# A filter network laid out on 128 partitions, its arrays the first load and its biases inside the vector of constants

## The reference, cut to what matters

```python
HY_EMB, HY_FFN = 33, 64
def hyena_filter(L, w1, b1, w2, b2, w3, b3, w4, freq):
    ...
    z = jnp.concatenate([t_unit[:, None], jnp.cos(ang[:, None] * f), -jnp.sin(ang[:, None] * f)], axis=-1)
    h = jnp.sin(freq[0] * (z @ w1 + b1))
    h = jnp.sin(freq[1] * (h @ w2 + b2))
    h = jnp.sin(freq[2] * (h @ w3 + b3))
    h = (h @ w4).astype(jnp.float32)
    ...
    return k * lax.rsqrt(jnp.sum(k * k, axis=0, keepdims=True) + 1e-6)
```

## Time and profile before

| | |
|---|---|
| device time, 3 runs | median 2309.72 us (2306.71 to 2310.96) |
| the profiled execution's own time | 2304.54 us |
| its span | 2302.7 us |
| busy: TensorE / VectorE / ScalarE / GpSimd | 93% / 38% / 20% / 36% |
| mean granted TensorE clock | 0.955 of full speed |
| DMA over the span | 182.33 MB, mean 79 GB/s |

### The profile page before, as it was taken

How to read it: one execution, slowest core, us unless ns; L and a number is a source line. 1 busy time by engine, 2 the same in 40 slices (tenths; PEclk the granted TensorE clock), 3 DMA queues, 4 the chain that set the end, 5 groups by cost and what they waited for, 6 DMA issues and landing times.

```text
span 2302.7 us, 30202 instructions
## 1 busy us (share of the span) xinstructions
PE 2143.3 (93%) x11970; PEld 1710.9 (74%) x11970; DVE 869.8 (38%) x1249; ACT 451.3 (20%) x847; POOL 819.3 (36%) x439
## 2 busy tenths in 40 slices
PE   7989988999989978989999999997879998999997
PEld 3568657887877757878888888885656676888886
DVE  4543544212337774332121112233236664322334
ACT  3331111001344551031110001102005612100110
POOL 1443536121217765243222222224210034444442
PEclk8999998999989989989999999997889999999998
DMA  9434322333110011112111211122110012323222
GB/s 359 168 100 152 110 101 96 115 135 126 56 65 1 1 37 55 60 37 69 64 47 63 73 65 64 50 65 75 59 37 1 1 64 65 97 79 108 97 76 74
DMA packets 50840, 182.33 MB, mean 79 GB/s; under 512 B 5680, under 2 KB 5936, under 8 KB 49712
## 3 DMA queue, kind: packets, MB, share of 16 engines
q1 hardware_dynamic: 49296, 171.53, 22.1%
q10 hardware_dynamic: 928, 6.37, 0.8%
q0 software_dynamic: 512, 2.95, 0.4%
HBM read 178.72 MB, written 2.10 MB: 79 GB/s over the span
## 4 chain that ended last, share of the span: by engine, by line
PE 86%; DVE 6%; POOL 3%; ACT 2%; DMA 1%; issue 1%; ACTq 0%; DVEq 0%; SPq 0%; POOLq 0%
PE psum L512 21%; PE psum L517 21%; PE psum L513 21%; PE psum L1100 2%; PE psum L1088 2%; PE psum L1117 2%; PE psum L733 1%; PE psum L699 1%; PE psum L579 1%; PE psum L918 1%; POOL weights_lo L2129 1%; PE psum L943 1%; PE psum L535 1%; PE psum L662 1%; PE psum L541 1%
## 5 line engine op out<-in xcount | busy, mean ns | idle before, releaser
L2129 POOL TENSOR_TENSOR weights_lo<-weights,weights_hi 128x1024 fp32r<-128x1024 f32 (+1 forms) x232 | 515.4, 2222 | 1038.2 <-DVE weights_hi L1618 1038.2
L1618 DVE CAST weights_hi<-weights 128x1024 fp32r<-128x1024 f32 (+1 forms) x232 | 167.9, 725 | 919.8 <-PE psum L517 749.2
L517 PE MATMUL psum<-normed_lo,weights_hi 128*128 128x512 f32 x1760 | 508.6, 352 | 0.0
L512 PE MATMUL psum<-normed_hi,weights_hi 128*128 128x512 f32 x1088 | 394.0, 362 | 7.9 <-POOL weights_lo L2129 7.9
L513 PE MATMUL psum<-normed_hi,weights_lo 128*128 128x512 f32 x1088 | 375.3, 360 | 0.0
L517 PEld LDWEIGHTS psum<-normed_lo,weights_hi 128*128 128x128 f32 x1760 | 286.0, 190 | 16.7
L512 PEld LDWEIGHTS psum<-normed_hi,weights_hi 128*128 128x128 f32 x1088 | 205.8, 189 | 57.9 <-POOL weights_lo L2129 5.7
L512 PE MATMUL psum<-normed_first_hi,weights_hi 128*128 128x512 f32 (+1 forms) x672 | 234.1, 348 | 11.9 <-POOL weights_lo L2129 11.4
L513 PEld LDWEIGHTS psum<-normed_hi,weights_lo 128*128 128x128 f32 x1088 | 206.6, 190 | 36.1 <-issue 1.8
L513 PE MATMUL psum<-normed_first_hi,weights_lo 128*128 128x512 f32 (+1 forms) x672 | 214.6, 340 | 0.0
L512 PE MATMUL psum<-hidden_hi,weights_hi 128*128 128x512 f32 (+1 forms) x528 | 189.0, 358 | 0.0
(11 more groups left out here) (303 smaller groups left out, 3039.8 us busy)
## 6 DMA issues: line engine op xcount, KB each, us to landing
weights<-in_wall SPq DMA_DIRECT2D x264, 512.0 KB, 3.9
weights<-in_wall SPq DMA_DIRECT2D x32, 384.0 KB, 3.2
weights<-in_wall SPq DMA_DIRECT2D x32, 320.0 KB, 3.1
residual<-in_xT SPq DMA_DIRECT2D x1, 3072.0 KB, 14.3
residual<-in_xT ACTq DMA_DIRECT2D x1, 3072.0 KB, 9.8
phase<-in_tab ACTq DMA_DIRECT2D x2, 1280.0 KB, 5.5
out_T<-normed SPq DMA_DIRECT2D x2, 1024.0 KB, 4.3
normed<-in_window SPq DMA_DIRECT2D x1, 1536.0 KB, 8.7
```

The source lines that it names most:

```text
L512: mm(acc[:, lo:hi], WH[:, b, k, :], high[:, lo:hi], start=st, stop=False)
L517: ins = mm(acc[:, lo:hi], WH[:, b, k, :], low[:, lo:hi], start=False, stop=en)
L1618: dve.tensor_copy(WH[:, b, 0:n, :], W[:, s, HALF * b:HALF * b + n, :]).then_inc(w_hi, 1)
L2129: TT(WL[:, s, at, :], W[:, s, at, :], WH[:, b, 0:width(gs[0], b), :].bitcast(f32), ALU.subtract).then_inc(w_lo, 1)
```

## The change

The arrays of the network are packed for 128 partitions: the first 384 positions' features on partitions 0 to 63, the other 384 on 64 to 127, the weights on both. Layers 0 and 1 then work on tiles of 128 partitions by 384 tokens, and the two matmuls of a layer read and write different halves of the partitions. In layer 2 each matmul reads one half and writes all 128 partitions, as before. The load of these arrays (128 x 768 floats, 384 KB, as many bytes as before) becomes SyncE's first DMA. Frequencies and biases are six more columns of V, and their own load is gone; VectorE's product of the two now waits for V.

```diff
-               ("hcw", 3 * 24), ("hcb", 24), ("dskip", 8), ("cc", 16), ("sel", 2), ("sink", 16), ("dtb", 32), ("alog", 32),
+               ("hcw", 3 * 24), ("hcb", 24), ("dskip", 8), ("cc", 16), ("sel", 2), ("sink", 16), ("dtb", 32), ("alog", 32), ("hyf", 3), ("hyb", 3),
...
-        HF = [KS[:, 0, 2 * n:2 * n + 2, 512:896] for n in range(3)]
-        ZT = KS[:, 1, 0:2, 512:896]
-        W1S, W2S, W3S = KS[:, 1, 2, 512:576], KS[:, 1, 2, 576:640], KS[:, 1, 2, 640:768]
-        FBV = KS[:, 1, 3, 512:521]
+        HF = [KS[:, 0, 0, 512:896], KS[:, 0, 1, 512:896], KS[:, 0, 4:6, 512:896]]
+        ZT = KS[:, 1, 0, 512:896]
+        W1S, W2S, W3S = KS[:, 1, 1, 512:576], KS[:, 1, 1, 576:640], KS[:, 1, 1, 640:768]
+        FBV = KS[:, 1, 3, 512:515]
...
+                if at == 0:
+                    sp.dma_start(KS[:, 1, 0:2, 512:896], A["hy_mlp"].rearrange("p (a b) -> p a b", a=2)) \
+                        .then_inc(small_in, 16)
                 if at == 3:
                     sp.dma_start(W4[:, :], A["hy_w4"]).then_inc(w4_in, 16)
                     sp.dma_start(C[:, :, :], A["const"].rearrange("p (a b) -> p a b", a=7)).then_inc(c_in, 16)
...
-            pe.wait_ge(small_in, 32)
+            pe.wait_ge(small_in, 16)
             for layer in range(3):
                 if layer:
                     pe.wait_ge(mlp_sin, layer)
                 for a in range(2):
+                    side = slice(64 * a, 64 * a + 64)
                     if layer == 0:
-                        ins = mm(PS[0:64, a, 0:384], W1S[0:HY_EMB, :], ZT[0:HY_EMB, a, :], start=True, stop=True)
+                        ins = mm(PS[side, 0, 0:384], W1S[64 * a:64 * a + HY_EMB, :], ZT[64 * a:64 * a + HY_EMB, :],
+                                 start=True, stop=True)
                     elif layer == 1:
-                        ins = mm(PS[0:64, a, 0:384], W2S[0:64, :], HF[0][0:64, a, :], start=True, stop=True)
+                        ins = mm(PS[side, 0, 0:384], W2S[side, :], HF[0][side, :], start=True, stop=True)
                     else:
-                        ins = mm(PS[:, a, 0:384], W3S[0:64, :], HF[1][0:64, a, :], start=True, stop=True)
+                        ins = mm(PS[:, a, 0:384], W3S[side, :], HF[1][side, :], start=True, stop=True)
                 ins.then_inc(mlp_mm, 1)
                 fill()
...
             act.dma_start(V[:, 0:VEC_W - 2], A["vec"]).then_inc(v_in, 16)
-            act.dma_start(KS[0:64, 1, 0:3, 512:D], A["hy_mlp"].rearrange("p (a b) -> p a b", a=3)).then_inc(small_in, 16)
-            act.dma_start(FBV[:, 0:6], A["hy_fb"]).then_inc(small_in, 16)
-
             act.wait_ge(v_in, 16)
             act.wait_ge(eps_ready, 2)
             run(CS[:, :, 0:2], V[:, _cols["cc"]:_cols["cc"] + 16].rearrange("p (k c) -> p k c", c=2),
@@ -1186,14 +1188,13 @@
 
 
             for layer in range(3):
-                n = 64 if layer < 2 else P
                 act.wait_ge(mlp_mm, layer + 1)
 
                 act.wait_ge(fb_ready, 1)
-                run(HF[layer][0:n, :, :], PS[0:n, 0:2, 0:384], Id, scale=FBV[0:n, layer:layer + 1],
-                    bias=FBV[0:n, 6 + layer:7 + layer]).then_inc(mlp_arg, 1)
+                run(HF[layer], PS[:, 0:2, 0:384] if layer == 2 else PS[:, 0, 0:384], Id, scale=vec("hyf", layer),
+                    bias=FBV[:, layer:layer + 1]).then_inc(mlp_arg, 1)
                 act.wait_ge(mlp_red, layer + 1)
-                run(HF[layer][0:n, :, :], HF[layer][0:n, :, :], ACT.Sin).then_inc(mlp_sin, 1)
+                run(HF[layer], HF[layer], ACT.Sin).then_inc(mlp_sin, 1)
                 copy_row([AT["ada_a"] + 2 * layer], 0)
                 if layer == 0:
                     act.wait_ge(w4_in, 16)
...
-            dve.wait_ge(small_in, 32)
-            TT(FBV[:, 6:9], FBV[:, 0:3], FBV[:, 3:6], ALU.mult).then_inc(fb_ready, 1)
+            dve.wait_ge(v_in, 16)
+            TT(FBV, vec("hyf", 0, 3), vec("hyb", 0, 3), ALU.mult).then_inc(fb_ready, 1)
...
             for layer in range(3):
                 dve.wait_ge(mlp_arg, layer + 1)
-                n = 64 if layer < 2 else P
-                h, q = HF[layer][0:n, :, :], halves(T[0:n, 0, :], 2)
+                h, q = HF[layer], T[:, 0, 0:384] if layer < 2 else halves(T[:, 0, :], 2)
                 ch.link(TS(q, h, 1.0 / (2 * float(np.pi)), MAGIC, ALU.mult, ALU.add))
                 ch.link(TS(q, q, MAGIC, None, ALU.subtract))
                 ch.link(STT(h, q, -TWO_PI_HI, h, ALU.mult, ALU.add))
@@ -2456,17 +2456,18 @@
...
+    put("hyf", np.tile(a["hy_freq"][0].T, (2, 1)))
+    put("hyb", np.tile(np.stack([a["hy_b1"][0], a["hy_b2"][0], a["hy_b3"][0]], 1), (2, 1)))
     wdt = hy[:, D + XBC_BLKS * P:h0]
-    mlp = np.zeros((64, 3, 512), np.float32)
-    mlp[0:HY_EMB, 0:2, 0:384] = _features().reshape(HY_EMB, 2, 384)
-    mlp[0:HY_EMB, 2, 0:64] = a["hy_w1"][0]
-    mlp[:, 2, 64:256] = np.concatenate([a["hy_w2"][0], a["hy_w3"][0], a["hy_w3"][0]], 1)
+    mlp = np.zeros((2, 64, 2, 384), np.float32)
+    mlp[:, 0:HY_EMB, 0] = _features().reshape(HY_EMB, 2, 384).transpose(1, 0, 2)
+    mlp[:, 0:HY_EMB, 1, 0:64] = a["hy_w1"][0]
+    mlp[:, :, 1, 64:256] = np.concatenate([a["hy_w2"][0], a["hy_w3"][0], a["hy_w3"][0]], 1)
     w4 = a["hy_w4"][0]
-    fb = np.concatenate([a["hy_freq"][0].T, np.stack([a["hy_b1"][0], a["hy_b2"][0], a["hy_b3"][0]], 1)], 1)
...
-        "hy_mlp": mlp.reshape(64, 3 * 512), "hy_fb": np.concatenate([fb, fb], 0),
+        "hy_mlp": mlp.reshape(P, 2 * 384),
```

## The result

The changed kernel takes 2289.95 us (median of 4 runs, 2289.23 to 2291.41), the kernel before 2308.22 (4 runs, 2306.3 to 2310.96). The changed kernel's profiled execution took 2289.23 us, its span is 2287.4, 15.3 less than before.

The account below looks back on a forecast made before the run. The prediction took the small network's ladder before the filter product as the reachable limit, then W4 and ada weight landings. 6.7 us earlier less 0.7 for clock gave 6.0 us: 2303.7 against 2309.72, range 2299.8 to 2309.0.

Parts of the forecast that it names:

- Start of layer 0 near 6.0: Head of the kernel: with its arrays loaded first, layer 0 starts on TensorE near 6.0 instead of 12.05 us.
- W4 at 16.1, scaled copy 1 at 17.2, 3.6 us a layer, sine 1 at 20.8: ScalarE's negation waits for the W4 load, delaying scaled copy 1; sine 1 ends at 20.8 instead of 27.70, 6.9 us sooner.
- Matmul halves overlap: Network layers: halves on different array rows run together; layer 2's 2.94 us could shrink to about 1.6, nothing booked.
- Ada weights are late, the product starts at 29.8: Before the filter product: TensorE waits for pair 2's ada weights, so it begins at 29.8 instead of 36.48, 6.7 us earlier.
- Half clock costs 0.7 us: Start of the filter product: half clock reaching 1.5 us into it loses 0.75 us; 0.7 subtracted.
- The parts are not worth their sum; nothing in the DMA queue is late behind 29.8: Head: 6.0 and 2 us leave 4.9 at scaled copy 1; after the filter product starts, the queue has room.
- The rest of the kernel waits only for its own engines, and I let it move as a block.: Everything after the head: it keeps its own duration and shifts earlier with the filter product.
- 6 columns (3 KB) in the vector: Load of the vector of constants: the biases add 6 columns, 3 KB, to it.
- rivals: Slower DMA (chance 0.22), half clock in the filter product (0.10 small, 0.06 slower), worthless front load (0.06), more than forecast (0.12).
- more than forecast: Rival: W4 sooner, queue at 0.419 MB per us, filter product at 28.7, no clock loss: 7.8 us, 2301.9; chance 0.12.
- The closing sentence of the prediction: Wrong if the filter product begins at 29.8 and the in-projection's first product at 125.55 is not also some 6 us earlier.

Follow-up runs that it names:

- two runs of single parts: Only the new loads, and only the layout on 128 partitions, each at the old addresses, against the kernel before: 2301.4 and 2301.72 us, both ratio 0.9974.
- The pad alone: The kernel before with 32 unused bytes per partition in front of temps, nothing else different: 2298.47 us, ratio 0.9966 to the kernel before.

## Why the prediction was wrong

By its own steps:

- *Start of layer 0 near 6.0.* It was 4.46; the forecast had it 1.5 us too late. The vector was in 2.5 us after its issue in the changed kernel and the network's arrays 3.6; I had let the vector land where it landed before. It did not matter, since W4 came behind it (16.01).
- *W4 at 16.1, scaled copy 1 at 17.2, 3.6 us a layer, sine 1 at 20.8.* Measured 16.01, 17.09, 3.6, 20.68.
- *Matmul halves overlap.* Layer 2's took 1.65 us instead of 2.94; 1.6 was the estimate.
- *Ada weights are late, the product starts at 29.8.* Right in kind and size: 29.6, held by the landing of the last half of pair 2's weights (28.50).
- *Half clock costs 0.7 us.* It did not: L667 took 10.65 us. That such a price exists is shown by the run with the window behind the ada jobs, 1.7 us.
- *The parts are not worth their sum; nothing in the DMA queue is late behind 29.8.* The first is confirmed at the filter product by the two runs of single parts (5.3 us each, 5.9 together), not by their times. For the second, the lead is 6.9 us at the filter product and still 6.3 at 119.24.
- *"The rest of the kernel waits only for its own engines, and I let it move as a block."* This is the step that failed, together with the one that booked the six columns as "6 columns (3 KB) in the vector", that is as bytes on the queue, and put nothing for what lies behind them in memory. They are also 24 bytes in front of every tensor behind them. The rest of the kernel did not move as a block: its matmuls got another pitch, in the second layer 2.4% shorter. The pad alone shows it: 0.34%, and the change without the shift 0.42%. Against the 6.0 us forecast, the change at the old addresses gave 7.0 us of span and 9.7 by its ratio (interval 6.2 to 12.9).

None of the rivals had this mechanism either; "more than forecast" reached 7.8 us and meant the DMA queue. The closing sentence of the prediction asked for the wrong sign to look at: the in-projection did start some 6 us earlier, and still something downstream had a time of its own. That the filter product came at 29.6 where 29.8 was forecast is in part luck: at the old addresses the same head had it at 30.61, with the same waits.

What stays open: why the 128 bytes matter, why it takes both sides, and why the first layer's feed-forward, with its matmuls of 512 and 256 columns in turn, follows the places otherwise than the second's with 512 alone. The low parts of the weights and of the normed activations lie on multiples of 128 in every run. So no run tells whether the high parts have to be on a multiple of 128 themselves or only at the same place as the low parts. And it is not shown whether the 2.8 us that the change at the old addresses lost behind the attention are scatter of the clock: the two runs of single parts lost them there too, the one kept trace of the kernel before did not.

## What to carry to other kernels

When an edit makes a tensor longer, list what is allocated behind it and compare the addresses before comparing anything else: here 24 bytes of constants were worth 0.34%, and all that the edit was about 0.42%. A pad of a few bytes is the cheapest experiment there is, and in a kernel bound by TensorE it is worth trying for its own sake, with the count of matmuls in a fixed stretch as the measure. The stretch must hold no wait: with phase 64 bytes higher than before, 1930 to 2100 holds one and gives 168.25 busy us over 723 matmuls, 0.2327 us each, where 2045 to 2200 gives 0.2307. At a start where the DMA queue is full, cost two shortenings of one ladder together and against the landings behind it: at the filter product each of the two parts gave 5.3 us alone and both gave 5.9 to 6.9.

## What the runs showed of the hardware

The pitch of fp32r matmuls of 128x512 at full clock depended on where their operands lie in SBUF. With stationary and moving operands all on multiples of 128 bytes 684 or 685 passed in 155 us, in six kernels (0.2263 us). With phase, which holds the high parts, 96 bytes above a multiple of 128 it was 668 (0.2320), 32 or 64 bytes above it 672 (0.2307), and with only one side of the high parts on a multiple 666 (0.2327).

Matmuls that alternate 512 and 256 columns behaved otherwise. In 160 us of the first layer's up-projection 913 or 914 passed with phase 0 or 32 bytes above a multiple of 128, and 919 with it 64 or 96 above; 919 and 920 passed with only the stationary or only the moving high parts on a multiple of 128, but 914 with the moving high parts 64 bytes above and the stationary ones on it. None of these runs says why.
